# Hybrid attention and mixture-of-experts block: half of the expert weight loads issued from GpSimd's queue

## The reference

```
x = x + merged @ w_out                      # two attention branches, gated
h2 = rmsnorm(x, norm2_g)
top_v, top_i = lax.top_k(h2 @ w_router + b_router, 4)      # 4 of 32 experts
gates = softmax(top_v)
# for the tokens of each expert ex:
gu = xb @ w1[ex] + b1[ex]                   # w1[ex]: 1024 x 2048
gate = minimum(gu[:, :1024], 7.0); up = clip(gu[:, 1024:], -7.0, 7.0)
y = ((up + 1.0) * gate * sigmoid(gate * 1.702)) @ w2[ex] + b2[ex]   # w2[ex]: 1024 x 1024
x = x + sum over the 4 experts of gate weight * y
return rmsnorm(x, final_g)
```

## Time and profile before

| | |
|---|---|
| time, median of 3 runs | 1134.62 us (1134.04 to 1134.88) |
| the profiled execution's own time | 1134.65 us |
| its span | 1132.8 us |
| TensorE busy | 1077.8 us (95%) |
| VectorE, ScalarE, GpSimd busy | 285.9, 104.2, 11.2 us |
| moved by DMA | 436.35 MB, mean 385 GB/s over the span |
| TensorE's granted clock | 0.997 of full |

### The profile page before, as it was taken

The page is one execution under the profiler, slowest core; times in us unless marked ns, Lnnn a source line. Parts: engine busy times, 40 slices in busy tenths (PEclk is TensorE's granted clock), DMA queues, the critical chain, the costliest instruction groups (busy, mean ns, idle before and its releaser), DMA issues.

```text
span 1132.8 us, 13083 instructions
## 1 busy us (share of the span) xinstructions
PE 1077.8 (95%) x5173; PEld 477.6 (42%) x5173; DVE 285.9 (25%) x614; ACT 104.2 (9%) x221; POOL 11.2 (1%) x20
## 2 busy tenths in 40 slices
PE   8999999999999999999999999999999999999997
PEld 7888788633333333333333333333333333333332
DVE  4346412322222222222222222221211122222222
ACT  1130430200000000000000000000000000000001
POOL 1100000000000000000000000000000000000000
PEclk9999999999999999999999999999999999999999
DMA  9954257589999999999999999999999999999995
GB/s 357 420 220 148 85 213 333 200 350 429 427 428 429 429 428 429 428 429 428 429 428 429 428 429 429 428 429 428 429 429 429 428 429 428 429 428 429 428 425 231
DMA packets 34917, 436.35 MB, mean 385 GB/s; under 512 B 4336, under 2 KB 4848, under 8 KB 6896
## 3 DMA queue, kind: packets, MB, share of 16 engines
q1 hardware_dynamic: 33888, 435.10, 91.4%
q10 hardware_dynamic: 1008, 0.95, 0.2%
HBM read 434.98 MB, written 1.05 MB: 385 GB/s over the span
## 4 chain that ended last, share of the span: by engine, by line
PE 74%; DMA 18%; SPq 4%; DVE 3%; issue 1%; another core or an unknown queue 0%; ACT 0%; POOL 0%; POOLq 0%; DVEq 0%
PE bank L777 29%; DMA ring<-in_w 17%; PE bank L810 15%; PE bank L504 8%; PE bank L693 4%; PE bank L743 4%; SPq L349 4%; PE bank L699 3%; PE bank L618 2%; PE bank L600 2%; DVE work L1140 1%; PE bank L500 1%; PE bank L761 1%; PE bank L459 1%; PE bank L524 1%; PE bank L553 1%
## 5 line engine op out<-in xcount | busy, mean ns | idle before, releaser
L777 PE MATMUL bank<-ring,work 128*64 128x512 f32 x2048 | 450.9, 593 | 21.2 <-DMA ring<-in_w 20.6
L777 PEld LDWEIGHTS bank<-ring,work 128*64 128x64 f32 x2048 | 147.3, 137 | 304.1 <-issue 273.8
L810 PE MATMUL bank<-ring,work 128*64 128x512 f32 x1024 | 233.6, 598 | 18.1 <-DVE work L1140 18.1
L810 PEld LDWEIGHTS bank<-ring,work 128*64 128x64 f32 x1024 | 67.9, 136 | 141.1 <-issue 115.4
L1131 DVE TENSOR_SCALAR work<-bank 128x512 f32<-128x512 f32 x32 | 22.1, 692 | 415.5 <-PE bank L777 415.5
L504 PE MATMUL bank<-ring 128*128 128x256 f32 x432 | 96.5, 381 | 0.0
L1270 ACT ACTIVATE work<-work 128x512 f32<-128x512 f32 x32 | 20.1, 629 | 754.0 <-DVE work L1131 754.0
L504 PEld LDWEIGHTS bank<-ring 128*128 128x128 f32 x432 | 81.1, 190 | 13.2 <-issue 2.4
L693 PE MATMUL bank<-x2n,work 128*64 128x512 f32 x264 | 65.0, 614 | 0.8 <-DVE work L1047 0.8
L743 PE MATMUL bank<-work 64*128 64x512 f32 x256 | 63.6, 615 | 0.9 <-DVE work L1145 0.9
L1067 DVE TENSOR_TENSOR work<-bank,vec 128x256 f32<-128x256 f32 x64 | 24.2, 420 | 136.5 <-PE bank L699 136.5
(11 more groups left out here) (176 smaller groups left out, 447.1 us busy)
## 6 DMA issues: line engine op xcount, KB each, us to landing
ring<-in_w SPq DMA_DIRECT2D x190, 2048.0 KB, 40.3
ring<-in_w_in SPq DMA_DIRECT2D x16, 1024.0 KB, 24.4
ring<-in_w_out SPq DMA_DIRECT2D x4, 1024.0 KB, 4.7
ring<-in_w SPq DMA_DIRECT2D x3, 1024.0 KB, 45.9
ring<-in_w_up_a SPq DMA_DIRECT2D x2, 1024.0 KB, 10.0
ring<-in_w_up_b SPq DMA_DIRECT2D x2, 1024.0 KB, 6.8
ring<-in_na_rpb SPq DMA_DIRECT2D x1, 1536.0 KB, 19.1
ring<-in_w SPq DMA_DIRECT2D x2, 512.0 KB, 39.7
```

The costliest lines, as they stand in the source:

```text
L777: last = pe.matmul(bank[CAP * a:CAP * (a + 1), bk, :], kT, pairs[:, pair_of(par, k // 2), at + q * 512:at + (q + 1) * 512], start=False, s ...
L810: last = pe.matmul(bank[CAP * a:CAP * (a + 1), BH, :], fT, pairs[:, pair_of(par, c), at + a * 512:at + (a + 1) * 512], start=f == 0, stop= ...
```

## The change

GpSimd issues the blocks c = 1, 3 and 5 of the experts 2 to 29 (84 of the 192), in a loop of its own between its second and third call of `power`. Each waits for the same value of `chunk_used` as before. They report their landing on new semaphores, `odd_landed[par][c // 2]`. SyncE's loop over j keeps c = 0, 2 and 4. TensorE waits through a new function, `wait_pair`, for the semaphore that belongs to the block and the value it has there: for odd blocks of experts 2 to 29 `j * 16` on the new one; for those of experts 30 and 31, which SyncE still issues, 32 on the old one. `pair_source` moves to where both engines' code can call it.

```
+        odd_landed = [[sem(f"odd_landed{par}_{c}") for c in range(1, W1_CH + W2_CH, 2)] for par in range(2)]
...
             with sp.Fori(1, E // 2 - 1) as j:
                 for par in range(2):
-                    for c in range(BLK):
+                    for c in range(0, BLK, 2):
                         load_chunk(2 * j + par, c, par, (2 * j + par - 2) * BLK + (PRE + c + 1))
...
             power(1, slice(0, MT), 2)
+
+            with pool.Fori(1, E // 2 - 1) as j:
+                for par in range(2):
+                    for c in range(1, BLK, 2):
+                        pool.wait_ge(chunk_used, (2 * j + par - 2) * BLK + (PRE + c + 1))
+                        pool.dma_start(pairs[:, pair_of(par, c), :],
+                                       pair_source(2 * j + par, c)).then_inc(odd_landed[par][c // 2], 16)
 
             power(2, slice(0, 1), 3)
...
-            def expert_block(b, par, landings, first=False, last_one=False):
+            def wait_pair(par, c, landings, odd):
+
+                if c % 2 and odd[1]:
+                    pe.wait_ge(odd_landed[par][c // 2], odd[0])
+                else:
+                    pe.wait_ge(pair_landed[par][c], odd[0] if c % 2 else landings)
+
+            def expert_block(b, par, landings, odd, first=False, last_one=False):
...
-                        pe.wait_ge(pair_landed[par][k // 2], landings)
+                        wait_pair(par, k // 2, landings, odd)
...
-                        pe.wait_ge(pair_landed[par][c], landings)
+                        wait_pair(par, c, landings, odd)
...
-                    expert_block(2 * j + par, par, j * 16 + 16)
-            expert_block(E - 2, 0, E // 2 * 16)
-            expert_block(E - 1, 1, E // 2 * 16, last_one=True)
+                    expert_block(2 * j + par, par, j * 16 + 16, (j * 16, True))
+            expert_block(E - 2, 0, E // 2 * 16, (32, False))
+            expert_block(E - 1, 1, E // 2 * 16, (32, False), last_one=True)
```

More of the change, by code:

```diff
@@ L294, in pair_of, with pair_source @@
             return c if par else BLK + c
+        def pair_source(e, c, cols=slice(0, PAIR_F)):
+            w, at = (w1, c) if c < W1_CH else (w2, c - W1_CH)
+            return w[bass.ds(e, 1), at, :, cols].rearrange("e p n -> p (e n)")
         BLK = W1_CH + W2_CH
@@ L349, in load_chunk @@
                 sp.dma_start(pairs[:, pair_of(par, c), :], pair_source(blk, c)).then_inc(pair_landed[par][c], 16)
-            def pair_source(e, c, cols=slice(0, PAIR_F)):
-                w, at = (w1, c) if c < W1_CH else (w2, c - W1_CH)
-                return w[bass.ds(e, 1), at, :, cols].rearrange("e p n -> p (e n)")
             for n in range(1, PRE):
@@ L824, in _ @@
             turn_gathered()
-            expert_block(0, 0, 16, first=True)
-            expert_block(1, 1, 16)
+            expert_block(0, 0, 16, (16, False), first=True)
+            expert_block(1, 1, 16, (16, False))
             with pe.Fori(1, E // 2 - 1) as j:
                 for par in range(2):
-                    expert_block(2 * j + par, par, j * 16 + 16)
-            expert_block(E - 2, 0, E // 2 * 16)
-            expert_block(E - 1, 1, E // 2 * 16, last_one=True)
+                    expert_block(2 * j + par, par, j * 16 + 16, (j * 16, True))
+            expert_block(E - 2, 0, E // 2 * 16, (32, False))
+            expert_block(E - 1, 1, E // 2 * 16, (32, False), last_one=True)
             n_over = pe.value_load(ctrl[0:1, OVER:OVER + 1], min_val=0, max_val=OVER_MAX)
@@ L837, in _ @@
                     with pe.If(j < n_over):
-                        expert_block(j + E, 0, j * 16 + 16 * (E // 2 + 1))
+                        expert_block(j + E, 0, j * 16 + 16 * (E // 2 + 1), (j * 16 + 48, False))
                     pe.nop()
```

## The result

The changed kernel took 1136.36 us in the median (17 runs), the kernel before 1134.35 (17 runs); the ratio is 1.0019, 95% interval 1.0012 to 1.0025. That is 2 us, inside the 0.2% that the prediction calls "same", but slower beyond the interval. One of the 17 executions of the changed kernel, 1153.15 us at a granted clock of 0.945, was in a slower state and is left out of the ratio. Forecast: 1135.0. The profiled execution took 1136.36 us with a span of 1134.3 (before 1134.65 and 1132.8).

What follows compares the result with a forecast made beforehand. The prediction took the weight-load stream, at 428 or 429 GB/s from about 256 us on, to bound the kernel. 1134.6 us plus 0.4 for GpSimd's start, all else 0, gave 1135.0; own range 1133 to 1137, overall 1124 to 1146.

Steps and rivals of the forecast that it cites:

- the two costs: GpSimd's start of loads, +0.4 us (0 to 1), and the landing order of two queues, 0 (up to +1).
- What bounds the kernel: Weight loads at 429 GB/s, 29.35 us an expert, set the end; TensorE's own pace is 27.15.
- Part 1: Three of six issues leave SyncE; its long ones, up to 11.4 us, should go, worth nothing.
- Part 2: GpSimd's issues, hidden except where engines run dry at 252 to 256 us: +0.4 us, between 0 and 1.
- Part 3: Two queues change landing order; TensorE waits earlier, from a reserve spent anyway: 0 us, bounds 0 and +1.
- If they serve one more ... nothing at the end: If engines favour one queue, it leads by at most six slots; something stays queued, no cost at the end.
- Part 4: Semaphore waits and GpSimd's issues beside VectorE cost at most 2.1 us an expert, below the 2.2 reserve: no change.
- Gaps filled: Second queue fills an end-of-transfer gap of 0.09 us: up to 15 us faster, 1120, half 1127; chance 0.20.
- Lower rate: Second queue lowers the load rate: 1142, half 1138; 3.4 us more by the skill's 425 GB/s; chance 0.22.
- Cannot run ahead: GpSimd's 1024 descriptor bytes fit one transfer, so starts follow landings; a tenth uncovered gives 1158; chance 0.06.
- Compute slowed: GpSimd's issues cost over 2.2 us an expert on TensorE's path; at 3 us, 1157; chance 0.04.

Runs made afterwards that it cites:

- e3_early: The changed kernel with GpSimd issuing the odd blocks of experts 2 to 5 only, SyncE all others; 1136.48 us, 1.0015 of the kernel before.
- e6_stop: The changed kernel with GpSimd issuing the odd blocks of experts 2 to 25 only, SyncE all of 26 to 31; 1136.21 us, 1.0019 of the kernel before.
- e7_delay_all: The changed kernel with each of GpSimd's issues waiting for one block more to be used; 1141.87 us, 1.0064 of the kernel before.
- e10_delay_late: The changed kernel with GpSimd's issues waiting for one block more only from expert 10 on; 1136.31 us, 1.0021 of the kernel before.
- e4_actq: The changed kernel with ScalarE instead of GpSimd issuing the odd blocks of experts 2 to 29; 1135.46 us, 1.0008 of the kernel before.
- e9_allpool_end: The changed kernel with GpSimd issuing all blocks of experts 2 to 31, pieces included; 1136.64 us, 1.0022 of the kernel before.
- e2_late: The changed kernel with GpSimd issuing the odd blocks of experts 10 to 29 only, SyncE all of 2 to 9; 1147.20 us, 1.0108 of the kernel before.
- e11_experts: The changed kernel with GpSimd issuing all six blocks of odd experts 3 to 29, SyncE those of even ones; 1145.29 us, 1.0095 of the kernel before.
- e8_allpool: The changed kernel with GpSimd issuing all blocks of experts 2 to 29, SyncE those of 30 and 31; 1175.20 us, 1.0360 of the kernel before.
- e12_merged: The kernel before, all on SyncE, with blocks loaded two per transfer from expert 6 on; 1135.98 us, 1.0015 of the kernel before.
- e5_open2: The changed kernel with GpSimd issuing the odd blocks of experts 4 to 29, SyncE all of 2 and 3; 1137.19 us, 1.0028 of the kernel before.

## Why the prediction was right, and which steps were not

The total came out inside the forecast's own range of 1133 to 1137 us, and for the reason given first, a rate that a second queue leaves alone. That it lies so near the forecast is in part luck: the two costs were each put at 1 us at most, the early one measured 1.5 to 2.1, and the second, which other arrangements made 11 to 41 us, stayed hidden behind the first.

- **What bounds the kernel: right.** The end is the stream's end; the rate, both paces and the fixed end work came out as read.
- **Part 1, SyncE's long issues are worth nothing: right.** They went, but for one of 9.1 us, and the rate stayed.
- **Part 2, GpSimd's start costs 0.4 us, between 0 and 1: the time of the loss right, the place in it and the size not.** GpSimd is 0.54 us in an issue where SyncE is 0.33. The hole at 252 to 256 us did not grow, it shrank; the loss was in the windows around it, the first behind the hole at 230 to 234 us, which I had left out. It is 0.6 us by 264 us in the profile, 0.7 to 1.4 in the table above, and 2.1 in the medians of the two runs that have only this (e3_early, e6_stop). e7_delay_all and e10_delay_late show by a larger dose that a late issue costs bytes early and none late. That GpSimd's slower start is the cause, and not a second queue as such, is not shown: e4_actq lost as many bytes without GpSimd, e9_allpool_end lost 2.3 us without a second queue.
- **Part 3, order costs 0 to 1 us: about right for this change, wrong as reasoned.** The change lags 3.8 us late in the run, makes up all but 1.0, and that is hidden behind the last landing. It gets away with that where e2_late did not, whose second queue opened on one with six blocks, nor e11_experts, which does not alternate by block. "If they serve one more ... nothing at the end" fell in e2_late (13 us), e11_experts (11) and e8_allpool (41): the engines are never idle, but the reserve of TensorE that I counted as spent anyway is needed again at the end, where it can catch up only 2.2 us an expert. Single file until the last block (e9_allpool_end) took the 38 us back.
- **Part 4, the compute is untouched: right.** 27.15 us an expert with 26 of GpSimd's issues between 260 and 500 us. The Trainium skill's rule on the shared port ("SBUF — State Buffer", "Who interferes with whom") finds no trace here: VectorE's busy time moved by 0.01 us of 51.
- **Rivals.** *Gaps filled*: fell, and e12_merged shows no gap per transfer to fill. *Lower rate*: fell; the estimate of 3.4 us from the Trainium skill's 425 GB/s ("DMA: Bandwidth & Descriptors") does not fit the measured 428 or 429, even with everything on GpSimd's queue. *Cannot run ahead*: does not happen here, where six slots are at most on that queue and the ring holds seven; when the ring is full (e8_allpool), it costs through order, and not through starts, which is how I had it. *Compute slowed*: fell.

**Open:** 0.4 us of the first profile's difference; how much any second queue costs, as against GpSimd's; why e3_early and e6_stop lose 2.1 us in their medians, more than the 1.1 and 1.4 us of bytes in their profiles; why e5_open2's queues evened out. The expert stage itself begins at different times, its second block between 230.5 and 232.9 us over the profiles, which is more than what is left open.

## What to carry to other kernels

A second DMA queue brings no bandwidth where one keeps all engines busy, and it gives up the order: the engines served both queues side by side, not in order of issue. With six blocks in the first queue when the second opened, its blocks were late for the rest of the run (13 us); with two or so they evened out. If you need two, open the second while the first holds little, alternate in the order of use, and look at the last use, not at the DMA share. While the queues are short a late issue costs bytes. When compute runs only a little faster than the loads, a lag in landing order costs nothing while it lasts and is paid at the end.

## What the runs showed of the hardware that was not expected

- With 1024 bytes reserved, GpSimd's ring held seven transfers of 128 rows (landing 33.9 to 34.0 us, 4.89 us each, in e8_allpool and e9_allpool_end), and the eighth issue waited. SyncE's queue took about ten of them before its issues grew from 0.33 to 4 us.
- Two short waits of TensorE (0.49 and 1.11 us, 3.65 us of work between them) left its clock at full. In e5_open2 one wait of 1.86 or 1.87 us in the same place was followed by full speed in one expert (1019.20) and by 32 instructions in 8.79 instead of 7.09 us in another (1048.57), where the granted clock was 0.72 over 4 us, a mix of 2.4 and 1.2 GHz. So one longer wait in place of two short ones can cost almost its own length (1.7 us) once more.
